# A two-layer trunk of differential attention and gated DeltaNet: the softmax mix in one operation, and the decay's column part and beta on the activation engine

## The reference

```python
# group A, per head and block of 128 queries
s = jnp.einsum('bhmqd,bhmkd->bhmqk', q, k).astype(jnp.float32) * (A_HEAD_DIM ** -0.5)
p = jax.nn.softmax(s, axis=-1)
a = p[:, :, 0] - lam * p[:, :, 1]
o = jnp.einsum('bhqk,bhkd->bhqd', a.astype(v.dtype), v)

# group B, per head, direction and chunk; g is cumulated along the chunk
diff = g[..., :, None] - g[..., None, :]
decay = jnp.where(tri, jnp.exp(jnp.where(tri, diff, 0.0)), 0.0)
k_beta = k * beta[..., None]
m = jnp.einsum('bhncd,bhnsd->bhncs', k_beta, k) * decay
attn = jnp.einsum('bhncd,bhnsd->bhncs', q, k) * decay
```

## Time and profile before

| | us |
|---|---|
| median of the runs | 2796.25 |
| lowest and highest of three | 2790.44, 2798.44 |
| the profiled execution | 2790.21 |
| its span, first to last instruction | 2788.3 |
| PE busy | 2427.6 (87%) |
| DVE busy | 1493.9 (54%) |
| ACT busy | 842.3 (30%) |
| POOL busy | 403.6 (14%) |
| mean granted clock of PE | 0.942 |

### The profile page before, as it was taken

How to read it: one execution, slowest core, us unless ns; L and a number is a source line. 1 busy time by engine, 2 the same in 40 slices (tenths; PEclk the granted TensorE clock), 3 DMA queues, 4 the chain that set the end, 5 groups by cost and what they waited for, 6 DMA issues and landing times. The chain is left out here.

```text
span 2788.3 us, 41567 instructions
## 1 busy us (share of the span) xinstructions
PE 2427.6 (87%) x15126; PEld 1999.3 (72%) x15126; DVE 1493.9 (54%) x2406; ACT 842.3 (30%) x1415; POOL 403.6 (14%) x587
## 2 busy tenths in 40 slices
PE   6799999999898989897897698988988898987776
PEld 2377777777777878785776476867777786867775
DVE  1345556473737373745434647474746657474634
ACT  4433232323223232323112633223232323223223
POOL 0002111120203030302100003031212303030300
PEclk9999999999999999998999799999999998989898
DMA  9945352526253534334335143433232343333343
GB/s 336 340 110 143 84 145 59 159 64 167 65 152 80 141 91 131 86 110 148 96 118 178 57 129 86 104 79 102 64 104 76 104 103 84 103 88 112 103 123 109
DMA packets 553609, 329.82 MB, mean 118 GB/s; under 512 B 48658, under 2 KB 517814, under 8 KB 552710
## 3 DMA queue, kind: packets, MB, share of 16 engines
q1 hardware_dynamic: 526294, 285.71, 37.2%
q10 hardware_dynamic: 27120, 42.02, 4.6%
q0 software_dynamic: 64, 0.20, 0.0%
HBM read 304.73 MB, written 23.13 MB: 118 GB/s over the span
## 5 line engine op out<-in xcount | busy, mean ns | idle before, releaser
L1641 PE MATMUL ps<-h_hi,w_hi 128*128 128x512 f32 (+1 forms) x2080 | 848.0, 408 | 91.5 <-DVE w_lo L1007 76.9
L1642 PE MATMUL ps<-h_lo,w_hi 128*128 128x512 f32 (+1 forms) x2080 | 782.4, 376 | 0.0
L1643 PE MATMUL ps<-h_hi,w_lo 128*128 128x512 f32 (+1 forms) x2080 | 781.3, 376 | 0.0
L1007 DVE TENSOR_TENSOR w_lo<-w_raw,w_hi 128x1024 fp32r<-128x1024 f32 (+1 forms) x332 | 406.0, 1224 | 338.9 <-ACT w_hi L604 279.2
L1641 PEld LDWEIGHTS ps<-h_hi,w_hi 128*128 128x128 f32 x2080 | 410.2, 197 | 206.8 <-DVE w_lo L1007 84.2
L604 ACT CAST w_hi<-w_raw 128x1024 fp32r<-128x1024 f32 (+1 forms) x332 | 341.3, 1030 | 518.1 <-PE ps L1643 205.1
L1643 PEld LDWEIGHTS ps<-h_hi,w_lo 128*128 128x128 f32 x2080 | 409.2, 197 | 69.6
L1642 PEld LDWEIGHTS ps<-h_lo,w_hi 128*128 128x128 f32 x2080 | 412.0, 198 | 48.3
L1490 POOL TENSOR_SCALAR small<-small 128x4 f32<-128x4 f32 (+3 forms) x51 | 13.2, 259 | 2071.6 <-POOLq L132 1024.5
L1891 PE MATMUL ps<-h_hi,w_hi 128*128 128x512 f32 (+1 forms) x448 | 163.8, 366 | 48.0 <-DVE w_lo L1007 47.9
L1007 DVE TENSOR_TENSOR arena<-arena,ps 128x512 f32<-128x512 f32 x160 | 104.3, 685 | 100.5 <-PE ps L1723 99.6
(11 more groups left out here) (193 smaller groups left out, 3160.4 us busy)
## 6 DMA issues: line engine op xcount, KB each, us to landing
w_raw<-in_w_in SPq DMA_DIRECT2D x260, 512.0 KB, 5.3
ada_raw<-in_w_ada SPq DMA_DIRECT2D x148, 512.0 KB, 5.6
w_raw<-in_w_out SPq DMA_DIRECT2D x64, 448.0 KB, 3.9
w_raw<-in_w_ada SPq DMA_DIRECT2D x44, 512.0 KB, 7.0
arena<-decay_rows ACTq DMA_DIRECT2D x16, 512.0 KB, 5.0
x_channel_major<-arena ACTq DMA_DIRECT2D x1, 4096.0 KB, 16.9
mixed<-arena ACTq DMA_DIRECT2D x16, 256.0 KB, 2.2
arena<-x_channel_major ACTq DMA_DIRECT2D x16, 256.0 KB, 2.8
```

Source lines behind the costliest of these rows:

```text
L1007: return V.tensor_tensor(o, a, b, op)
L1641: mm(o, w_hi[:, s, k], h_hi[:, kt, t0:], start=kt == 0, stop=False)
L1642: mm(o, w_hi[:, s, k], h_lo[:, kt, t0:], start=False, stop=False)
L1643: last = mm(o, w_lo[:, s, k], h_hi[:, kt, t0:], start=False, stop=kt == KT - 1)
```

## The change

The softmax mix uses one full-width operation instead of two: with r0 and r1 the reciprocals of the sums s0 and s1, DVE forms the one column r1 * s0 * lambda, adds map 1 times it to map 0, and `oa_copy` multiplies the attention's product by r0 (a pointer operand) as it leaves PSUM. The decay's column part goes from DVE to ACT: the table holds the negated cumulated g, DVE only adds the mask to `g_row`, and ACT takes the exponential of each 128x128 group with its column as bias, eight groups in all. Then ACT multiplies each group by its beta column into `m_T`, again eight operations, and only then signals `decay_ready`. DVE forms `m_T` by one product per direction with the gram in PSUM, signals `m_ready`, and makes `att_T` after that.

```diff
--- before.py
+++ after.py
@@ -795,7 +795,18 @@
                         act.wait_ge(decay_arg, h())
                         need(act, ob_turned, h(-2))
                         own.go(nc.scalar.activation(q_dec[:, :, c0:], g_row[:, :, c0:], ACT.Exp))
-                        nc.scalar.activation(decay, decay, ACT.Exp).then_inc(decay_ready, 1)
+                        for d in range(2):
+                            for cc in range(NT):
+                                own.go(nc.scalar.activation(decay[:, d, cc], decay[:, d, cc], ACT.Exp,
+                                                            bias=hcol[:, TAB_G, d, cc:cc + 1]))
+                        own.settle()
+                        for d in range(2):
+                            for cc in range(NT):
+                                m = nc.scalar.activation(m_T[:, d, cc], decay[:, d, cc], ACT.Copy,
+                                                         scale=hcol[:, TAB_BETA, d, cc:cc + 1])
+                                if (d, cc) != (1, NT - 1):
+                                    own.go(m)
+                        m.then_inc(decay_ready, 1)
                         act.wait_ge(decay_ready, h())
                         own.settle()
                         if not (isinstance(i, int) and i == HEADS):
@@ -863,7 +874,8 @@
 
                     def oa_copy(n):
                         act.wait_ge(oa_product, nth_q(layer, i, -1, n + 1))
-                        nc.scalar.copy(o_a[:, q_tiles[layer][n]], bank(A1, P)).then_inc(oa_copied, 1)
+                        nc.scalar.activation(o_a[:, q_tiles[layer][n]], bank(A1, P), ACT.Copy,
+                                             scale=small[:, 38:39]).then_inc(oa_copied, 1)
                         act.wait_ge(oa_copied, nth_q(layer, i, -1, n + 1))
 
                     def oa_squares():
@@ -1145,6 +1157,7 @@
                                                tab[:, TAB_G].rearrange("p x c h -> p c x h")))
                         tt(decay[:, 0, 3, 0:64], ps[:, A1, 64:128], tabf[:, TAB_G], ALU.subtract).then_inc(tab_last, 1)
                         vec.wait_ge(tab_last, layer + 1)
+                        own.done(V.tensor_scalar(tabf[:, TAB_G], tabf[:, TAB_G], -1.0, None, ALU.mult))
 
                 def body(i, project, fill):
                     own.finish()
@@ -1205,8 +1218,7 @@
                                                .rearrange("p n o -> p (n o)")))
                         vec.wait_ge(g_loaded, h() * 16)
                         need(vec, ob_turned, h(-2))
-                        own.done(tt(decay, g_row, hcol[:, TAB_G].unsqueeze(3).to_broadcast([P, 2, NT, P]), ALU.subtract))
-                        tt(decay, decay, far.unsqueeze(2).to_broadcast([P, 2, NT, P]), ALU.add).then_inc(decay_arg, 1)
+                        tt(decay, g_row, far.unsqueeze(2).to_broadcast([P, 2, NT, P]), ALU.add).then_inc(decay_arg, 1)
                         vec.wait_ge(decay_arg, h())
 
                     def qk_sums():
@@ -1225,13 +1237,13 @@
                         vec.wait_ge(grams, h())
                         vec.wait_ge(decay_ready, h())
                         for d in range(2):
+                            own.go(tt(m_T[:, d], quads(G2), m_T[:, d], ALU.mult))
+                        own.settle()
+                        vec.sem_inc(m_ready, 1)
+                        for d in range(2):
                             own.go(V.scalar_tensor_tensor(att_T[:, d, c0:], quads(G3)[:, c0:], float(P) ** -0.5, decay[:, d, c0:],
                                                           ALU.mult, ALU.mult))
-                            for cc in range(NT):
-                                own.go(V.scalar_tensor_tensor(m_T[:, d, cc], quads(G2)[:, cc], hcol[:, TAB_BETA, d, cc:cc + 1],
-                                                              decay[:, d, cc], ALU.mult, ALU.mult))
                         own.settle()
-                        vec.sem_inc(m_ready, 1)
 
                     def substitute_backward(n):
 
@@ -1327,9 +1339,9 @@
                         keys = T if qt >= 2 else N_CTX
                         vec.wait_ge(exped, nth_q(layer, i, -1, n + 1))
                         own.done(V.reciprocal(small[:, 38:40], small[:, 36:38]))
-                        own.done(V.tensor_scalar(prob[:, 1, 0:keys], prob[:, 1, 0:keys], small[:, 39:40], lam[:, layer:layer + 1],
+                        own.done(V.tensor_scalar(small[:, 39:40], small[:, 39:40], small[:, 36:37], lam[:, layer:layer + 1],
                                                  ALU.mult, ALU.mult))
-                        V.scalar_tensor_tensor(prob[:, 0, 0:keys], prob[:, 0, 0:keys], small[:, 38:39], prob[:, 1, 0:keys],
+                        V.scalar_tensor_tensor(prob[:, 0, 0:keys], prob[:, 1, 0:keys], small[:, 39:40], prob[:, 0, 0:keys],
                                                ALU.mult, ALU.add).then_inc(mixed, 1)
                         vec.wait_ge(mixed, nth_q(layer, i, -1, n + 1))
```

## The result

The changed kernel takes 2820.19 us (median of 5 runs, 2815.40 to 2827.23), the kernel before 2794.52 us (5 runs, 2790.44 to 2798.44). The ratio is 1.0092, 95% interval 1.0078 to 1.0107: slower by 0.9%. The forecast was 2817 us. The profiled execution took 2818.93 us, its span is 2817.1 us, 28.8 more than before.

The account below looks back on a forecast made before the run. PE's fixed-order work, waits and halved clock were taken as the bound. Heads +9.1, -0.8 and +0.4, output stages +3.3, clock +8.5 made +20.5 us on 2790.2; with 6.0 to the median, 2817 us, range 2797 to 2842.

Parts of the forecast that it names:

- softmax exponentials: On ACT before mix 0: they start 4.0 us later in layer 0 and 3.4 later in layer 1.
- mix 0: The head's first query tile's softmax mix, awaited by PE: 2.5 us later in layer 0, 1.2 in layer 1.
- halved clock behind it: PE after its wait for mix 0: drops of 1.7 us, five in layer 0, +8.5 us; nothing more in layer 1.
- chain after the grams: DVE from the grams to the w_lo PE awaits: 1.2 us a head less in layer 0, 1.15 in layer 1.
- the rest: Later in the head: mixes 2 and 3 of layer 0 save 0.2 us each, counted as -0.8 us in all.
- output stages: Two stages with the heads' chain before their mix: +1.4 us in the first, +1.9 in the second, +3.3 together.
- The pieces: ACT's eight exponentials and eight copies of 128x128: 0.30 us apart, 5.0 us in all against 1.04 for one exponential.
- Rivals 2 and 3: ACT's pieces dearer, 0.40 us each, 2843 us, chance 0.12; or cheaper, 0.20 us each, 2781 us, chance 0.08.
- the relief beside POOL: DVE's w_lo and mix 0, slow beside POOL's L1520, come later: mix 0.66 us shorter, layer 1's w_lo 0.66 too.
- Rival 1: Same chain, but no drop of PE's clock behind mix 0: +12.0 us, 2808 us, chance 0.20.
- mix 1: The second query tile's mix on DVE, after the grams: 0.4 us less a head.
- Rival 4: Time doesn't move, 2796 us: what PE loses at mix 0 it gets back at later waits; chance 0.12.

Follow-up runs that it names:

- e8: The kernel before with thirteen copies of 128x128 added on ACT ahead of the decays' exponential, results overwritten; 2839.52 us, ratio 1.0168.
- e11: The kernel before with one wait added on POOL, which scales the keys only when mix 0 is done; 2764.89 us, ratio 0.9891.
- e4: The changed kernel with five unused multiplications ahead of PE's wait for mix 0 in layer 0; 2805.53 us, ratio 1.0029 to the kernel before.
- e9: The changed kernel with the signal m_ready put behind att_T, as in the kernel before; 2818.68 us, ratio 1.0081 to the kernel before.
- e1: The kernel before with the mix part alone: one full-width operation, the normaliser at the product's copy; 2762.62 us, ratio 0.9883.
- e3: The changed kernel with the decays moved behind qk_copy in ACT's plan; 2764.89 us, ratio 0.9888 to the kernel before.
- e7: e1 with the decays, still one wide exponential, moved behind qk_copy in ACT's plan; 2761.74 us, ratio 0.9889 to the kernel before.
- e2: The changed kernel with the mix part undone, so the decay part alone; 2828.72 us, ratio 1.0115 to the kernel before.

## Why the prediction was right, and where a term was off

The forecast of the sum was +20.5 us, the medians differ by 25.7 and the profiled executions by 28.7. That 2817 lies only 3 us below the measured 2820.19 is in part luck: the sum was added to a median of 2796.25 for the kernel before, which two more runs moved to 2794.52. By the profiled executions the sum was 8.2 us short: 3.8 in layer 0, 2.6 in layer 1, and 2.1 ahead of the first head, where almost nothing changed, less 0.2 in the output stages. Term by term, per head, measured in the stage table as changed kernel less before:

| term | forecast | measured |
|---|---|---|
| softmax exponentials, layer 0 / 1 | +4.0 / +3.4 | +3.87 / +3.31 |
| mix 0 on PE, layer 0 / 1 | +2.5 / +1.2 | +2.27 / +1.13 |
| halved clock behind it, layer 0 / 1 | +1.2 (8.5 / 7) / 0 | +1.48 / +0.43 |
| chain after the grams, layer 0 / 1 | -1.2 / -1.15 | -0.69 / -1.27 |
| the rest, layer 0 / 1 | -0.1 / 0 | -0.13 / +0.14 |
| seven heads, layer 0 / 1, us in all | +16.8 / +0.4 | +20.6 / +3.0 |
| output stages, first / second, us in all | +1.4 / +1.9 | +3.0 / +0.1 |

**The pieces.** Bounded between 0.27 and 0.40 us apart, taken as 0.30, measured 0.305. The pointer's 0.1 us, taken from two different groups, came out as well: the product's copy went from 267 ns to 367 with its scale (L877). Rivals 2 and 3 end here. The fixed cost that the Trainium skill's page VectorE: DVE Perf Modes (the section on the TRN2 errata) gives made an estimate of 4.7 us for the sixteen in the prediction; the trace shows 4.92, with each piece 390 ns long (L805) and begun 0.305 us after the one before. The 267 ns that the prediction set beside it are of a copy that reads PSUM.

**Mix 0.** The price of ACT's time, less the dropped operation and the relief beside POOL, came out within 0.25 us in both layers. e8 shows the price with the old mix: softmax exponentials 4.08 us later make mix 0 2.76 later in layer 0, and 3.53 make 1.62 in layer 1, what is missing being the relief. e11 shows the relief by itself, 1.91 us in layer 1.

**The clock.** Rival 1 is out: six of the seven heads of layer 0 have the halved clock behind mix 0 and none had it before, and where e4 fills the wait it is gone. A drop costs 1.73 us on the mean of the six (5.55 against 3.82), forecast 1.7; there were six and not five, 10.4 us in layer 0 for the 8.5. That the drop comes behind waits above some size is not borne out: the shortest of the seven waits was followed by it and a longer one was not.

```profile
259.34 1.11 PE L1808 MATMUL ps<-cst,arena 128*128 128x128 f32 x4 [2.65 <-DVE arena L1344]
...
1011.58 0.66 PE L1808 MATMUL ps<-cst,arena 128*128 128x128 f32 x4 [3.00 <-DVE arena L1344]
```

In layer 1 I had counted nothing, and it cost 0.43 a head, 3.0 us; the other terms of layer 1 cancel.

**The output stages** fit only as a sum. The first lost 3.0 us where I had 1.4, the second 0.1 where I had 1.9; that the two errors cancel is luck. The halved clock, for which I had put nothing there, shows in the first: its granted clock fell from 0.90 to 0.87 (the windows above), and e4, with the wait filled, has it 5.6 us shorter. Why the second came out at 0.1 was not looked into.

**The chain after the grams in layer 0** is the term that was mis-sized: half of the -1.2 was missing. DVE gained 1.0 of it; the gram terms take 2.74 us and not 2.6 (the prediction's own pieces would even give 2.45: two of 0.685 and two of 0.69, less three overlaps of 0.1), and mix 1 gave 0.3 for 0.4. In the head shown, from its first gram term to the start of its substitution (L295) it took 717.77 - 702.91 = 14.86 us before and 729.38 - 715.52 = 13.86 after. The w_lo behind the substitution then began 25.80 and 25.49 us after the first gram term, so 0.7 of the 1.0 was lost within it. This head and the next are those that lost most: over the seven the substitution takes 11.07 us before and 11.39 after, 0.32 lost, with nothing lost in the first two heads and 0.3 in three others. DVE and POOL in the substitution, kernel before:

```profile
719.99 1.48 DVE L295 TENSOR_TENSOR arena<-arena 32x24 f32<-32x24 f32 x1
...
723.35 1.05 DVE L301 TENSOR_TENSOR arena<-arena 32x512 f32<-32x512 f32 x1
...
725.14 1.54 DVE L301 TENSOR_TENSOR arena<-arena 32x512 f32<-32x512 f32 x1
...
719.90 1.53 POOL L301 TENSOR_TENSOR arena<-arena 32x512 f32<-32x512 f32 x1
...
723.56 2.21 POOL L301 TENSOR_TENSOR arena<-arena 32x512 f32<-32x512 f32 x1
```

And the changed kernel:

```profile
731.14 1.55 DVE L295 TENSOR_TENSOR arena<-arena 32x30 f32<-32x30 f32 x1
...
734.99 2.23 DVE L301 TENSOR_TENSOR arena<-arena 32x512 f32<-32x512 f32 x1
...
737.96 1.21 DVE L301 TENSOR_TENSOR arena<-arena 32x512 f32<-32x512 f32 x1
...
731.12 1.52 POOL L301 TENSOR_TENSOR arena<-arena 32x512 f32<-32x512 f32 x1
734.79 1.53 POOL L301 TENSOR_TENSOR arena<-arena 32x512 f32<-32x512 f32 x1
```

Before, DVE's L301 began at 723.35 and POOL's at 723.56: DVE had 1.05 us and POOL 2.21. After, POOL's began first, 734.79 against 734.99: POOL had 1.53 and DVE 2.23. The earlier `m_ready`, which I had priced at nothing, moved POOL's half to 8.4 us after the first gram term where it had begun at 10.3, and with it which engine comes second. e9 moves the signal back, and on the mean the substitution takes 10.86 us; in layer 1, where this meeting falls otherwise, it takes 11.10 for 11.33 and the term came as forecast. That the order of the two engines makes the 0.3 us is read from these rows; which order a head falls into was not predicted and is not explained.

**Rival 4**, that PE gets its loss back at later waits, is half true in layer 1: of 1.56 lost up to the grams 1.27 came back. In layer 0 it was 0.69 of 3.75.

**The w_lo waits**, to which the prediction gave no change, grew by 2.4 us in all. Behind the grams DVE's chain sets when that w_lo comes; mix 1 now comes earlier in it, PE's wait for mix 1 shrinks from 3.21 to 2.23 us, and most of that goes over to the wait for w_lo, 2.70 to 3.39.

## What to carry to other kernels

Work moved to an engine with 30% load is not free: ask what stands behind it in that engine's order up to the next thing that the bounding engine waits for, and put it behind that. Here the same sixteen operations, with what they save on DVE, cost 58 us in one place (the changed kernel against e1) and nothing in another (e3 against e7). Two edits that relieve the same operations need not add; and before a DVE operation is made shorter, look whether it is only slow because of what POOL runs beside it, since one wait on POOL was worth as much as the rewritten mix.

## What the runs showed of the hardware

In these rows an operation of DVE with two inputs in SBUF that begins while a wide one of POOL, also with two, is under way does not run slowly, it stands still until POOL is done: the 32x30 L295 of DVE, 0.18 us otherwise, began at 731.14 and ended at 732.69, POOL's L301 ran from 731.12 to 732.64. The other way round it holds as well, as e9's rows show, with a 0.69 us operation of DVE that started first:

```profile
730.92 0.69 DVE L1193 SCALAR_TENSOR_TENSOR arena<-arena 128x512 f32<-128x512 f32 x1
731.64 1.35 DVE L295 TENSOR_TENSOR arena<-arena 32x14 f32<-32x14 f32 x1
...
731.04 1.93 POOL L301 TENSOR_TENSOR arena<-arena 32x512 f32<-32x512 f32 x1
```

POOL, 0.12 us behind, took 1.93 instead of 1.53, and the next DVE operation then waited for POOL's end (732.97 against 732.99). The Trainium skill's page SBUF — State Buffer (section SBUF: two separate sides) says so: the pair of ports that the two engines share is an exclusive lock, and for a DVE operation with two SBUF inputs against a POOL one that reads SBUF, whoever starts first has it for the whole instruction. By that rule, the trace agrees.

A halved clock behind mix 0 cost 1.73 us a time in layer 0 (changed kernel), measured up to the end of the grams. What a head gains or loses beyond that is not shown to come from the clock. Where DVE and POOL meet in the substitution moves it as well: on the mean of layer 0 that stretch took from 10.86 us (e9) to 11.66 (e2), and it accounts for 0.45 of the 2.0 us a head that e4 gives.
